# Moving the query-transpose steps inside the windowed-attention head loop of a two-layer encoder kernel

## The reference

```
def trunk(x, mem, p):
    for i in range(DEPTH):
        h = rmsnorm(x, p['norm_in'][i])
        ...
            z = h @ p['b_w_in'][j]
            q, k, v, q_mem, gate = jnp.split(z, SPLIT_B, axis=-1)
            mix = swa_mixer(q, k, v, p['b_q_norm'][j], p['b_k_norm'][j], p['b_sink'][j])
        mem_o = memory_attention(q_mem, mem, p['mem_norm'][i], p['w_mem_kv'][i], ...)
        branch = jnp.concatenate([mix, mem_o], axis=-1) * jax.nn.silu(gate)
        x = x + branch @ p['w_out'][i]

    # inside swa_mixer, for a block i of 128 queries
        s = jnp.einsum('bqkgd,bjkd->bkgqj', q_blk, k_blk).astype(jnp.float32) * scale
        s = jnp.where(valid, s - slopes * dist, NEG)
        sk = jnp.broadcast_to(sink_l, s.shape[:-1] + (1,))
        p = jax.nn.softmax(jnp.concatenate([s, sk], axis=-1), axis=-1)[..., :-1]
        return jnp.einsum('bkgqj,bjkd->bqkgd', p.astype(v_blk.dtype), v_blk)
```

## Time and profile before

| | before |
|---|---|
| time, median of 3 runs | 1434.75 us (1434.05 to 1436.62) |
| the profiled execution's own time | 1434.05 us |
| its span in the profile | 1432.3 us |
| TensorE busy | 1393.2 us (97%) |
| VectorE busy | 981.5 us (69%) |
| ScalarE busy | 760.0 us (53%) |
| GpSimd busy | 412.8 us (29%) |
| matmuls | 8120 |

### The profile page before, as it was taken

The page is one execution under the profiler, slowest core; times in us unless marked ns, Lnnn a source line. Parts: engine busy times, 40 slices in busy tenths (PEclk is TensorE's granted clock), DMA queues, the critical chain, the costliest instruction groups (busy, mean ns, idle before and its releaser), DMA issues.

```text
span 1432.3 us, 23084 instructions
## 1 busy us (share of the span) xinstructions
PE 1393.2 (97%) x8120; PEld 1236.3 (86%) x8120; DVE 981.5 (69%) x2072; ACT 760.0 (53%) x1823; POOL 412.8 (29%) x535
## 2 busy tenths in 40 slices
PE   7999999999999999999999999999999999998999
PEld 6889889898888888798888898899888888887997
DVE  6555687887655647888664656888877556578883
ACT  7354466555544436666463535656655345366661
POOL 2231252330202223734212213422311112246450
PEclk9999999999999999999999999999999999999999
DMA  6413221114341222222262132121133413122222
GB/s 224 119 49 88 77 69 46 43 50 146 118 133 55 78 71 82 62 65 90 96 198 82 50 94 79 51 62 47 38 103 126 121 49 96 58 77 60 67 71 103
DMA packets 88674, 121.47 MB, mean 85 GB/s; under 512 B 10353, under 2 KB 58865, under 8 KB 88561
## 3 DMA queue, kind: packets, MB, share of 16 engines
q1 hardware_dynamic: 83088, 112.31, 25.9%
q10 hardware_dynamic: 5472, 7.69, 1.8%
HBM read 115.77 MB, written 4.19 MB: 84 GB/s over the span
## 4 chain that ended last, share of the span: by engine, by line
PE 72%; DVE 12%; ACT 9%; issue 4%; POOL 2%; ACTq 1%; DMA 0%; SPq 0%; DVEq 0%; POOLq 0%
PE bank L1509 22%; PE bank L1511 21%; PE bank L1510 21%; PE bank L1555 5%; ACT prob L578 4%; DVE bank L1270 3%; DVE w_lo_t L881 3%; DVE probT L889 2%; POOL rr L1340 1%; ACT w_hi L553 1%; PE bank L1515 1%; PE bank L1516 1%; ACT q_st L575 1%; DVE nmax L1274 1%; POOL rtmp L1339 1%
## 5 line engine op out<-in xcount | busy, mean ns | idle before, releaser
L881 DVE TENSOR_TENSOR w_lo_t<-w_raw,w_hi 128x256 fp32r<-128x256 f32 (+3 forms) x540 | 302.1, 575 | 288.4 <-ACT w_hi L553 276.0
L553 ACT ACTIVATE w_hi<-w_raw 128x256 fp32r<-128x256 f32 (+3 forms) x544 | 268.5, 509 | 334.3 <-PE bank L1511 310.2
L1509 PE MATMUL bank<-w_hi,actT 128*128 128x256 f32 (+3 forms) x1120 | 361.5, 323 | 5.5 <-DVE probT L889 3.4
L1510 PE MATMUL bank<-w_lo_t,actT 128*128 128x256 f32 (+3 forms) x1120 | 359.1, 321 | 0.0
L1509 PEld LDWEIGHTS bank<-w_hi,actT 128*128 128x128 f32 x1120 | 212.5, 190 | 21.7 <-DVE w_lo_t L881 5.6
L1510 PEld LDWEIGHTS bank<-w_lo_t,actT 128*128 128x128 f32 x1120 | 212.6, 190 | 14.3
L1393 POOL TENSOR_TENSOR prob<-prob,rinv 128x256 f32<-128x256 f32 x192 | 137.9, 748 | 283.7 <-DVE rinv L987 283.7
L1511 PE MATMUL bank<-w_hi,brlo 128*128 128x256 f32 (+1 forms) x608 | 189.0, 311 | 0.0
L578 ACT ACTIVATE prob<-bank,nmax 128x256 f32<-128x256 f32 (+2 forms) x256 | 138.3, 551 | 79.3 <-DVE nmax L1181 39.7
L1511 PE MATMUL bank<-w_hi,actT 128*128 128x512 f32 (+3 forms) x512 | 170.1, 332 | 0.0
L1509 PE MATMUL bank<-actT,w_hi 128*128 128x512 f32 x384 | 152.8, 398 | 3.9 <-DVE probT L889 2.3
(11 more groups left out here) (141 smaller groups left out, 2710.7 us busy)
## 6 DMA issues: line engine op xcount, KB each, us to landing
w_raw<-in_w_mem SPq DMA_DIRECT2D x64, 256.0 KB, 2.6
w_raw<-in_w_out SPq DMA_DIRECT2D x112, 128.0 KB, 2.1
w_raw<-in_w_b SPq DMA_DIRECT2D x112, 128.0 KB, 2.1
w_raw<-in_w_b SPq DMA_DIRECT2D x48, 256.0 KB, 2.7
w_raw<-in_w_out SPq DMA_DIRECT2D x40, 256.0 KB, 2.8
w_raw<-in_w_a SPq DMA_DIRECT2D x32, 256.0 KB, 2.7
w_raw<-in_w_a SPq DMA_DIRECT2D x64, 128.0 KB, 2.0
bias<-in_alibi ACTq DMA_DIRECT2D x28, 192.0 KB, 2.3
```

The source lines that it names most:

```text
L553: act.activation(w_hi[:, n % SPLIT, 0:width], w_raw[:, n % RAW, 0:width], ACT.Copy).then_inc(w_hi_done, 1)
L881: dve.tensor_tensor(w_lo_t[:, n % SPLIT, 0:width], w_raw[:, n % RAW, 0:width], w_hi[:, n % SPLIT, 0:width].bitcast(fp32), ALU.subtract).th ...
L1509: nc.tensor.matmul(out, lhs[0], rhs[0], start=start, stop=False, skip_group_check=skip)
L1510: nc.tensor.matmul(out, lhs[0], rhs[1], start=False, stop=False, skip_group_check=skip)
```

## The change

Six pieces of code are put in another order. Nothing is added or taken away.

In the head loop, the query and key transposes move later. On TensorE, and in `plan()`, `b_q` and `b_k` go behind `b_o(h)`. On ScalarE their high parts go behind `b_exp(h + 2)`. On VectorE their low parts go behind `gated`, the second `fill`, and `b_p(h + 2)`, directly ahead of `b_pt(h + 1)`.

```
@@ plan() @@
                 fill(stream, WINDOW_FILL[h][0])
+                take([("bO", L, h)])
                 if h % 2 == 0 and h + 4 < HB:
                     take([("bqT", L, h // 2 + 2)])
                 if h + 3 == HB // 2:
                     take([("bkT", L, 1)])
-                take([("bO", L, h)])
@@ ScalarE @@
                             fill(WINDOW_FILL[h][0])
+                            if h + 2 < HB:
+                                b_exp(h + 2)
                             if h % 2 == 0 and h + 4 < HB:
                                 b_q(h // 2 + 2)
                             if h + 3 == HB // 2:
                                 b_k(1)
-                            if h + 2 < HB:
-                                b_exp(h + 2)
                             fill(WINDOW_FILL[h][1])
@@ VectorE @@
                             if h + 2 < HB:
                                 b_max(h + 2)
+                            gated(("bO", L, h), h // 2, half(h % 2))
+                            fill(WINDOW_FILL[h][1])
+                            if h + 2 < HB:
+                                b_p(h + 2)
                             if h % 2 == 0 and h + 4 < HB:
                                 b_q(h // 2 + 2)
                             if h + 3 == HB // 2:
                                 b_k(1)
-                            gated(("bO", L, h), h // 2, half(h % 2))
-                            fill(WINDOW_FILL[h][1])
-                            if h + 2 < HB:
-                                b_p(h + 2)
                             if h + 1 < HB:
                                 b_pt(h + 1)
@@ TensorE @@
                             fill(WINDOW_FILL[h][0])
+                            b_o(h)
                             if h % 2 == 0 and h + 4 < HB:
                                 b_q(h // 2 + 2)
                             if h + 3 == HB // 2:
                                 b_k(1)
-                            b_o(h)
```

At the start of a layer pass, the splits of two weight tiles move ahead of the evictions of `memV`, on ScalarE and VectorE alike (`hi` and `w_hi_to` here, `lo` and `w_lo_to` there):

```
+                    w_hi_to(FIRST["memK", L, NM - 1] + SPLIT)
                     for j in range(NM):
                         use = ("memV", L, j)
                         hi(use, v0[:, 0, 2 * j:2 * j + 2, :], bank(use)[:].rearrange("p (a b) -> p a b", a=2))
-                    w_hi_to(FIRST["memK", L, NM - 1] + SPLIT)
```

More of the change, by code:

```diff
@@ L1027, in _ @@
                         w_lo_to(FIRST["memV", L, NM - 1] + SPLIT + 3 + i)
+                    w_lo_to(FIRST["memK", L, NM - 1] + SPLIT)
                     for j in range(NM):
@@ L1031, in _ @@
                            v0[:, 0, 2 * j:2 * j + 2, :])
-                    w_lo_to(FIRST["memK", L, NM - 1] + SPLIT)
                     for k in range(KD):
@@ L1300, in _ @@
                                 b_k(1)
[L1301 to L1304, removed]
                             if h + 1 < HB:
```

## The result

| | before | after |
|---|---|---|
| time, median | 1434.83 us (1434.05 to 1436.62, 4 runs) | 1486.62 us (1484.06 to 1488.89, 4 runs) |
| ratio to before, 95% interval | | 1.0358 [1.0339, 1.0379] |
| profiled execution, its span | 1434.05 us, 1432.3 us | 1491.49 us, 1489.7 us |
| mean granted clock of TensorE | 1.00 | 0.978 |
| head loop 1, first to last `nmax` | 113.0 us | 140.9 us |

The forecast was 1472 us with a range up to 1484: the direction was right, the size was not. The time is 2.6 us above the range. The profiled execution is the longest of after; over its runs the time goes with the clock (a span of 1482.3 us at 0.986, of 1487.1 and 1489.7 us at 0.978).

What follows compares the result with a forecast made beforehand. The prediction took a ring of VectorE and ScalarE to bound the head loop: 36.4 us for two loops plus 0.4 us at layer-pass starts, 36.8 us in all, gave 1472 us; range 1454 to 1484 us.

Steps and rivals of the forecast that it cites:

- What bounds the kernel: Head loop: VectorE and ScalarE wait for each other in a cycle, 8.19 us in pass 0; TensorE has 0.3 us slack.
- The ring: Head loop: VectorE's maxima, ScalarE's exponentials and two weight splits, VectorE's low parts, next maxima; 18.2 us longer per loop.
- ScalarE's eviction: Even head-loop passes: query high parts now stand between exponentials and weight splits, adding 1.27 us; bounds 0 and 1.39.
- VectorE's eviction: Even head-loop passes: query low parts now stand between the reciprocal and the probabilities' low parts, adding 1.54 us.
- Rival 1: Head loop: only VectorE's half counts; VectorE instructions stretched beside GpSimd might not be in other phases; 1455 us, chance 0.16.
- pass 5: Odd head-loop pass with the key eviction in the same new places on ScalarE and VectorE: 1.3 us longer.
- TensorE and the banks: Head loop: TensorE up to about 2 us behind in odd passes, catches up in the next; 0 taken, bounds 0 and 24 us.
- rival 2: Head loop: TensorE's clock falls in the new waits, 1.24 us in each of 12; say 1483 us, chance 0.12.
- Start of a layer pass: TensorE's 0.93 us wait stays or moves before the last transposes; 0.1 us each, 0.4 us for four passes.

Runs made afterwards that it cites:

- experiment 7: Kernel before, with one ScalarE weight split per head-loop pass moved ahead of the exponentials: 1426.23 us, 0.9950.
- experiment 9: Kernel before, with only VectorE's part of the head loop (and the banks) in the changed order: 1464.44 us, 1.0200.
- experiment 10: Kernel before, with VectorE's and ScalarE's parts of the head loop changed, TensorE's order and the layer-pass start as before: 1486.80 us, 1.0358.
- experiment 6: The kernel of experiment 5 with 59 extra matmuls a head loop, results overwritten, ahead of six scores: 1478.75 us, 1.0314.
- experiment 5: Kernel after, with the planner's lag of the query and key transposes' banks (bqT, bkT) raised to 4.0: 1483.96 us, 1.0353.
- experiment 2: Kernel after, with ScalarE and VectorE back in the old head-loop order; TensorE's order, banks and layer-pass start stay changed: 1440.26 us, 1.0047.

## Why the forecast was wrong

**What bounds the kernel: right.** The ring of VectorE and ScalarE sets the pace of the head loop. Experiments 7 and 9 turn it both ways.

**ScalarE's eviction, 1.27 us an even pass: right.** Measured 1.27 in pass 0 (4.73 - 3.46), and passes 0, 8 and 10 of experiment 10 against 9 are 1.28, 1.27 and 1.26 us longer.

**VectorE's eviction, 1.54 us: too small by 0.12 to 0.15.** Behind the reciprocal it does not start as closely as `probT` did. An undisturbed even pass is 2.95 us longer, 17.7 us for six instead of 16.9.

**What VectorE is stretched by, not in the sum.** Rival 1 named it, but as a possible gain. In passes 8 and 10 a weight split falls beside GpSimd's `brlo` and takes 1.24 us, where it took 0.42 before. VectorE's rows of pass 10 before, then after, then GpSimd's after:

```profile
657.16 0.42 DVE L881 TENSOR_TENSOR w_lo_t<-w_raw,w_hi 128x256 fp32r<-128x256 f32 x1
...
659.43 0.69 DVE L1274 TENSOR_SCALAR nmax<-mx,sinks 128x4 f32<-128x4 f32 x1
```

```profile
684.87 1.24 DVE L881 TENSOR_TENSOR w_lo_t<-w_raw,w_hi 128x256 fp32r<-128x256 f32 x1
...
687.96 0.23 DVE L1274 TENSOR_SCALAR nmax<-mx,sinks 128x4 f32<-128x4 f32 x1
```

```profile
684.54 1.29 POOL L1373 TENSOR_TENSOR brlo<-gate,actT 128x512 fp32r<-128x512 f32 x1
```

That is 0.8 us twice a loop. More than half of it comes back: before, `brlo` fell on the `nmax` behind these passes (0.69 us instead of 0.23), and passes 9 and 11 of experiment 6 are 0.47 us shorter than before. In its loop 1 the six even passes grow by 20.0 us (17.7 of the two evictions, 1.7 of the stretched splits, 0.6 in passes 2 and 4), where I had summed 16.9. The other passes grow by 1.3 us on balance, the forecast's figure, but by luck: pass 5 takes 0.76 us instead of 1.3, passes 1, 3 and 7 take 1.5 that I had at 0, and passes 9 and 11 give 0.9 back. With 21.3 and 21.7 us instead of 18.2 a loop, this is 6.6 us of the miss.

**TensorE and the banks: "I take 0" is the step that failed.** I had seen that the scores would wait for VectorE's late low part, and that TensorE would be up to 2 us behind. Then I let it catch up in the next pass, with its work lasting "8.19 us and a little more" a pass. That holds where the clock does (pass 7 of loop 2 below). But the wait itself can take the full clock away, so that the work of catching up lasts longer: odd passes 1 to 9 take 9.64 to 11.9 us, where they had 8.05 to 9.85, but for that pass 7. The lag then ends up in the ring, as VectorE's 11.8 us of waits for TensorE's head outputs. This is **rival 2**, to which I gave 0.12. Its price was about 11 us (1483 instead of 1472). In the profiled executions the loops of after stand 12.6 us above those of experiment 6; in the medians, each against its own before, it is 51.8 against 45.8, so 6.0 us. Experiment 6 has 27 us more work, so the clock may cost more than that. That 11 lies between the two is in part luck: I had 1.24 us lost in each of 12 waits, but the mean clock of 0.978, against 0.999 before, is an estimated 31 us lost in the span, 2.6 a wait, of which more than half fell into time that TensorE had to spare. The price had to be added to a ring of 43 us and not of 36.4.

The trace had told of it, by the earlier trace rows, though I misread where this stretch stands: between the wait of 7.4 us and it TensorE made transposes for 3.3 us and waited another 1.8 us, and the clock was 1.00 up to 12 us. I weighed against it waits of up to 1.0 us, which were no evidence for waits of 2 to 4.

The same kernel shows the step at one place in both its states. Passes 6 and 7 of loop 1 are in the table above: clock 0.85, then 9.64 us. In loop 2 the clock happened to hold in the same wait:

```profile
1369.51:1380.66 11.15, 8.68 (x70) 1.00 0.18 55
1380.66:1388.70 8.04, 8.04 (x66) 1.00 0.24 75
```

Then pass 7 is 8.04 us, as before the change. The ring gives 11.15 in both, and the waits are 2.48 and 2.47 us; only the clock behind them differs. In loop 1 TensorE's head output then comes late, VectorE waits for it and for the transposes, and a weight split stands beside GpSimd (0.81 us instead of 0.41): 1.6 us of the odd pass in all. The Trainium skill, "TensorE: Matmul & The Clock Gate", section "Why this matters for your kernels", says to leave no idle gaps between bursts of matmuls, as they bring the clock down. The runs agree for the waits of 3.1 us and more, all of which were followed by the lower level (0.39 to 0.63 us for the same matmul behind the 3.7 us of pass 0); at 1.9 to 3.1 us they show both outcomes.

**Start of a layer pass: right.** TensorE's wait of 0.93 us in the earlier trace rows has moved in front of the last transposes, as said:

```profile
397.75 0.33 PE L1624 MATMUL bank<-ident,prob 128*128 128x128 f32 x1 [0.61 <-DVE v L889]
```

**The sum.** Forecast 36.4 + 0.4 = 36.8 us. Measured in the profiled execution: ring 43.0, the clock and the lag that it makes 12.6, the rest of the span 1.7, together 57.4 (rounded). The medians of the runs differ by 51.8, as the profiled execution was the longest: 45.8 of them are there in experiment 6 too, 9.0 more than the forecast, and 6.0 are not. So the step that failed is shown, but how the miss divides between it and the ring's own term depends on the execution. The range was too narrow as well: it cut off the upper part of rival 2 while the ring's own term could move up by a few us.

**What stays open.** How the 12.6 us divide between the clock and TensorE's lag behind a late bank: experiment 5 against after changes both, and is 6.3 us faster in the profiled loops, but no faster against its own before (1.0353 and 1.0358). And what decides, in waits of 1.9 to 3.1 us, whether the clock falls.

## What to carry to other kernels

Ask of an instruction not how long it takes but in whose shadow it stands: 2 x 1.4 us of evictions cost nothing while the ring was on the other engine, and 2.95 us a pass when they stood in it. When a change makes the matrix engine wait, add the price of its clock behind each new wait, and do not let it "catch up" at full speed. And once a ring across two engines is found, shorten it: one weight split moved out of it made this kernel 0.5% faster.

## What the runs showed of the hardware

- Each of the 37 waits of TensorE of 3.1 us or more, in the head loops of all twelve traces, was followed by the lower of the two clock levels: in pass 0 after, a matmul of 512 columns took 0.63 us instead of 0.39. After waits of 1.9 to 3.1 us it came both ways, also in one and the same place of one kernel (2.48 us and 0.85 in pass 6 of loop 1, 2.47 us and 1.00 in loop 2). After those of up to 1.0 us in the loops of before, and of up to 1.9 us in those of experiment 2, never; but once the clock fell behind two waits close together, of 1.0 and 1.5 us (pass 8 in loop 2 of experiment 5).
- Work done in vain can pay: 59 extra matmuls a loop made the kernel 5.2 us faster (experiments 5 and 6).
- VectorE's difference of two tiles in SBUF took 1.24 us instead of 0.42 when it started 0.33 us after a GpSimd operation of 1.29 us on SBUF; it ended 0.28 us behind that one. The Trainium skill, "SBUF — State Buffer", section "Who interferes with whom", says that a VectorE instruction with two inputs in SBUF and a GpSimd instruction that reads SBUF lock each other out, and that the second is blocked until the first is done. The row agrees with blocking rather than sharing: behind GpSimd's end VectorE needed 0.28 us, most of the 0.42 that it takes alone.
